# Late attention with the probabilities of seven head pairs transposed by VectorE in squares of 32 and exchanged through memory

## The reference, cut to what matters

```python
x = x + 0.5 * swiglu(rms_norm_2(x, ffn1_norm[l]), ffn1_w_gate[l], ffn1_w_up[l], ffn1_w_down[l])
h = rms_norm_2(x, mix_norm[l])
z = h @ w_in[l]
qa, ka, va, qs, ks_, vs, zg = jnp.split(z, splits, axis=-1)
...
o_na = neighbourhood_attention(qa, ka, va, na_rpb[l])
...
o_sw = sliding_window_gqa(qs, ks_, vs, t5_bias, sw_sink[l])
g = jax.nn.sigmoid((zg + b_gate[l]).astype(jnp.float32)).astype(x.dtype)
g = g.reshape(B, S, N_BRANCHES, D)
merged = g[:, :, 0] * (o_na @ w_branch_na[l]) + g[:, :, 1] * (o_sw @ w_branch_sw[l])
x = x + merged @ w_out[l]
x = x + 0.5 * swiglu(rms_norm_2(x, ffn2_norm[l]), ffn2_w_gate[l], ffn2_w_up[l], ffn2_w_down[l])
```

## Time and profile before

| | |
|---|---|
| time, median of 3 runs | 2544.74 us (2544.18 to 2547.61) |
| profiled execution | 2544.48 us |
| its span | 2543.2 us |
| mean granted clock of TensorE | 0.998 |
| TensorE busy | 2451.7 us (96%) |
| VectorE, ScalarE, GpSimd busy | 1249.2, 437.9, 178.7 us |
| moved by DMA | 712.90 MB, mean 280 GB/s |

### The profile page before, as it was taken

The page is one execution under the profiler, slowest core; times in us unless marked ns, Lnnn a source line. Parts: engine busy times, 40 slices in busy tenths (PEclk is TensorE's granted clock), DMA queues, the critical chain, the costliest instruction groups (busy, mean ns, idle before and its releaser), DMA issues.

```text
span 2543.2 us, 29763 instructions
## 1 busy us (share of the span) xinstructions
PE 2451.7 (96%) x12358; PEld 1567.5 (62%) x12358; DVE 1249.2 (49%) x2237; ACT 437.9 (17%) x1102; POOL 178.7 (7%) x126
## 2 busy tenths in 40 slices
PE   9999999888999999987889999999999999999999
PEld 5347443424578753332348866888866875888884
DVE  4994321212176621110117666545776775654774
ACT  2111110101123210000001002641101100470110
POOL 0011000000000000000000011430001003240000
PEclk9999999999999999999999999999999999999999
DMA  9854999999984499999999863415674974423671
GB/s 395 330 233 178 371 425 426 427 428 427 423 340 166 172 376 427 426 428 428 427 422 347 255 227 149 150 67 211 212 230 153 253 231 153 173 105 138 220 223 40
DMA packets 193618, 712.90 MB, mean 280 GB/s; under 512 B 117252, under 2 KB 121860, under 8 KB 128332
## 3 DMA queue, kind: packets, MB, share of 16 engines
q1 hardware_dynamic: 92304, 682.66, 67.6%
q10 hardware_dynamic: 101180, 28.35, 5.4%
HBM read 698.36 MB, written 12.60 MB: 280 GB/s over the span
## 4 chain that ended last, share of the span: by engine, by line
PE 79%; DMA 16%; DVE 4%; ACT 1%; issue 0%; POOL 0%; SPq 0%; another core or an unknown queue 0%; DVEq 0%; POOLq 0%
PE bank L867 77%; DMA ring<-in_stream 8%; DMA ring_high<-in_stream 4%; DMA ring_low<-in_stream 4%; PE bank L870 2%; DVE hidden L2892 1%; DVE ab_z L2717 1%; DMA hidden_turned<-normed 1%; DVE moe_results L2917 0%; POOL ab_ln_sum L3584 0%; DVE ring L3228 0%; DVE cd_y L2524 0%; DVE moe_turned L2913 0%; ACT normed L2243 0%; ACT hidden L2243 0%
## 5 line engine op out<-in xcount | busy, mean ns | idle before, releaser
L867 PE MATMUL bank<-ring,gates 128*128 128x256 f32 (+1 forms) x1760 | 433.6, 391 | 3.1 <-DVE ring L3228 2.1
L867 PE MATMUL bank<-ring,moe_chosen 128*64 128x512 f32 (+1 forms) x2352 | 400.3, 491 | 27.7 <-DMA ring<-in_stream 27.6
L867 PEld LDWEIGHTS bank<-ring,gates 128*128 128x128 f32 x1760 | 333.6, 190 | 70.7 <-issue 22.7
L867 PE MATMUL bank<-ring,normed 128*128 128x256 f32 x1448 | 339.6, 380 | 2.0 <-ACT normed L2328 1.3
L867 PEld LDWEIGHTS bank<-ring,moe_chosen 128*64 128x64 f32 x2352 | 150.6, 137 | 246.9 <-issue 200.4
L867 PEld LDWEIGHTS bank<-ring,normed 128*128 128x128 f32 x1448 | 273.1, 190 | 41.6 <-issue 3.9
L867 PE MATMUL bank<-normed,ring 128*128 128x256 f32 (+2 forms) x1152 | 289.8, 406 | 2.3 <-DVE normed L2698 1.5
L867 PEld LDWEIGHTS bank<-normed,ring 128*128 128x128 f32 x1152 | 189.4, 190 | 99.9 <-issue 85.4
L867 PE MATMUL bank<-ring,ffn_hidden 128*128 128x512 f32 (+1 forms) x416 | 179.3, 561 | 0.0
L2917 DVE COPY moe_results<-bank 32x512 f32<-32x512 f32 x36 | 24.8, 690 | 245.2 <-PE bank L867 244.8
L2908 DVE TENSOR_TENSOR moe_silu<-bank,moe_silu 128x512 f32<-128x512 f32 x32 | 22.1, 691 | 246.8 <-PE bank L867 246.8
(11 more groups left out here) (468 smaller groups left out, 2705.4 us busy)
## 6 DMA issues: line engine op xcount, KB each, us to landing
ring<-in_stream SPq DMA_DIRECT2D x318, 1024.0 KB, 7.3
ring<-in_stream SPq DMA_DIRECT2D x117, 2048.0 KB, 30.8
ring_low<-in_stream SPq DMA_DIRECT2D x7, 2048.0 KB, 43.8
ring_far<-in_stream SPq DMA_DIRECT2D x7, 2048.0 KB, 44.6
ring_high<-in_stream SPq DMA_DIRECT2D x6, 2048.0 KB, 44.8
hidden_turned<-normed ACTq DMA_DIRECT2D x44, 256.0 KB, 7.2
ffn_hidden<-hidden_turned ACTq DMA_DIRECT2D x44, 256.0 KB, 7.4
hidden<-in_stream SPq DMA_DIRECT2D x9, 1024.0 KB, 30.9
```

What stands on the lines that cost most here:

```text
L867: return nc.tensor.matmul(o, lhsT, rhs, start=start, stop=stop, skip_group_check=True)
```

## The change

The changed kernel no longer transposes the probabilities of pairs 0 to 6 on TensorE. `y.SC` becomes one block of 1024 columns in which the two heads' probabilities are laid out by pieces of 32 keys. After `probs(m)` VectorE transposes the whole block in squares of 32 into `y.turned`, a single buffer. SyncE then writes `y.turned` to memory in four pieces of 32 partitions and reads it back in the order of `y.PT` with two transfers (`probs_exchanged`). This stands in SyncE's order behind the refill of the place that the same pair's gate chunk has freed. The eighth pair is still transposed by TensorE. The values come three pairs after their scores (`LAG`) in place of two, and the order of VectorE's steps and that at the end of the stage are written anew. In each layer 56 transposes of TensorE and 14 copies of ScalarE go, and 7 transposes of VectorE, 28 writes and 14 reads come.

```diff
+    y.SC, y.turned = spare[:, 0:1024], spare[:, 1024:2048]
+    y.pairs = [M.ring[WEIGHT_SUMS[0]][:, SLOT + 1024 * n:SLOT + 1024 * n + 1024] for n in range(2)]
+    y.PT = [[x.rearrange("p (k i q) -> p i k q", k=TT, i=2)[:, i] for i in range(2)] for x in y.pairs]
...
+    def probs_exchanged(l, m):
+
+        sp.wait_ge(*S.vector.at(("turned_2", l, m)))
+        if m >= 2:
+            sp.wait_ge(*S.probs_in.at((l, m - 2)))
+        for q in range(4):
+            rows = bass.AP(tensor=probs_blocks[m % 2].tensor, offset=q * 32 * 1024, ap=[[128, 32], [32 * 128, 8], [1, 128]])
+            nc.sync.dma_start(rows, M.late.turned[32 * q:32 * q + 32, :].rearrange("p (k n) -> p k n", k=8)).then_inc(
+                *S.probs_out.up((l, m) if q == 3 else None))
+        sp.wait_ge(*S.probs_out.at((l, m)))
+        if m >= 2:
+            sp.wait_ge(*S.tensor.at(("values_2", l, m - 2)))
+        for k in range(TT):
+            rows = probs_blocks[m % 2].rearrange("(q k p x f) -> k p x q f", q=4, k=TT, p=P, f=32)[k]
+            to = M.late.pairs[m % 2].rearrange("p (k x q f) -> p k x q f", k=TT, q=4, f=32)[:, k]
+            nc.sync.dma_start(to, rows).then_inc(*S.probs_in.up((l, m) if k == TT - 1 else None))
+
+    gate_chunks = {ring.index["in_2", l, 9 + m] + 1: (l, m) for l in range(LAYERS) for m in range(NA_H - 1)}
...
             nc.sync.dma_start(to, src).then_inc(*ring.arrival(i).up(i if last else None))
+        if ring.to_be_free(i, n) in gate_chunks:
+            probs_exchanged(*gate_chunks.pop(ring.to_be_free(i, n)))
...
+VALUES_AT = (6,) * (NA_H - 1) + (7,)
+LAG = 3
...
-            for i in range(2):
-                pe.wait_ge(*A.at(("turned_2", l, m, i)))
+            pe.wait_ge(*(A.at(("turned_2", l, m, 1)) if m == NA_H - 1 else S.probs_in.at((l, m))))
...
         for m in range(pairs):
-            if m:
-                turned(m - 1)
             scores(m)
-            if m >= 2:
-                values(m - 2)
+            if m >= LAG:
+                values(m - LAG)
             gates_first(m)
             gates_rest(m)
             if m == 1:
                 keys_turned()
         turned(pairs - 1)
+        values(pairs - 3)
+        branch(0, 0)
+        branch(1, 0)
         values(pairs - 2)
-        branch(0, 0)
         values(pairs - 1)
-        branch(1, 0)
         branch(0, 1)
         branch(1, 1)
...
+        def turned(m):
+            dve.wait_ge(*done.at(("probs_2", l, m, 1)))
+            if m:
+                dve.wait_ge(*S.probs_out.at((l, m - 1)))
+            v.transpose(y.turned, y.SC).then_inc(*done.up(("turned_2", l, m)))
...
         for m in range(NA_H):
-            softmax(m)
+            if m:
+                gates_summed(m - 1)
+            biased(m)
+            if m:
+                gates_scaled(m - 1)
+            probs(m)
+            if m < NA_H - 1:
+                turned(m)
+            gates_first(m)
...
-            gates(m)
+        gates_summed(NA_H - 1)
+        gates_scaled(NA_H - 1)
```

More of the change, by code:

```diff
@@ L698, in wide, with probs_of, by_pieces @@
     return x.rearrange("p (o t) -> p o t", o=1).broadcast_to([P, n, x.shape[1]])
+def probs_of(y, m, i, t):
+    order = "i t k f" if m == NA_H - 1 else "k i t f"
+    return y.SC.rearrange(f"p ({order}) -> p i t k f", i=2, t=TT, f=32)[:, i, t]
+def by_pieces(x):
+    return x.rearrange("p (k f) -> p k f", f=32)
 def reversed_queries(x):
@@ L1895, in branch @@
                 pe.wait_ge(*V.at(("gated", l, p - 2, n)))
+            elif p:
+                pe.wait_ge(*A.at(("turned_2", l, NA_H - 1, n)))
             for half in range(2):
@@ L2483, in layer @@
                 keys_out()
+        values(NA_H - 3)
         turned(NA_H - 1)
+        gates(NA_H - 1)
         values(NA_H - 2)
-        gates(NA_H - 1)
         values(NA_H - 1)
@@ L3447, in keys_swapped, with biased @@
             v.tensor_copy(y.KSX[DH:P, :], y.KS[0:DH, :]).then_inc(*done.up(("ks_swapped", l)))
-        def softmax(m):
+        def biased(m):
             kind, blk = divmod(m, NA_H // 2)
@@ L3470, in softmax, with gate_parts, gates_first, gates_summed @@
                 for t in range(TT):
-                    v.tensor_scalar(y.SC[i][:, t, :], y.SC[i][:, t, :], total[:, t:t + 1], None, ALU.mult).then_inc(*done.up(("probs_2", l, m, i) if t else None))
-        def gates(c):
+                    part = probs_of(y, m, i, t)
+                    v.tensor_scalar(part, part, total[:, t:t + 1], None, ALU.mult).then_inc(*done.up(("probs_2", l, m, i) if t else None))
+        def turned(m):
[3 more added lines that the diff above has]
+            v.transpose(y.turned, y.SC).then_inc(*done.up(("turned_2", l, m)))
+        def gate_parts(c):
             b, d = (bank[x][:, :].rearrange("p (n t) -> p n t", t=P) for x in VALUES_BANK)
-            to = y.gates_of[c].rearrange("p (n t) -> p n t", t=P)
+            return b, d, y.gates_of[c].rearrange("p (n t) -> p n t", t=P)
+        def gates_first(c):
+            b, d, to = gate_parts(c)
             dve.wait_ge(*A.at(("gate_first", l, c)))
-            v.tensor_tensor(to[:, 0:4:3, :], b[:, 1:3, :], wide(to[:, 3, :], 2), ALU.add).then_inc(*done.up())
+            v.tensor_tensor(to[:, 0:4:3, :], b[:, 1:3, :], wide(to[:, 3, :], 2), ALU.add).then_inc(*done.up(("gate_firsts", l, c)))
+        def gates_summed(c):
+            b, d, to = gate_parts(c)
             dve.wait_ge(*S.chunk.at(("in_2", l, 9 + c)))
-            dve.wait_ge(*done.now())
+            dve.wait_ge(*done.at(("gate_firsts", l, c)))
             v.tensor_tensor(to[:, 1:3, :], d[:, 0:2, :], wide(to[:, 3, :], 2), ALU.add).then_inc(*done.up())
@@ L3613, in program @@
     pool_program(nc, a, M, S, ring)
-    every = [S.tensor, S.scalar, S.vector, S.pool, S.chunk, S.distance, S.spilled, S.hidden, S.sent, *S.landed, *S.into.values()]
+    every = [S.tensor, S.scalar, S.vector, S.pool, S.chunk, S.distance, S.spilled, S.hidden, S.probs_out, S.probs_in, S.sent, *S.landed, *S.into.values()]
     return {x.name: x.table for x in every}
```

39 lines of the change are left out of this document (19 added, 20 removed).

## The result

The changed kernel takes 2568.5 us (median of 5, 2565.78 to 2572.96) against 2545.1 (2544.18 to 2547.61): a ratio of 1.0094, 95% interval 1.0079 to 1.0109. It is 23.4 us slower, where 2547 was forecast and 2560 was the upper end.

What follows compares the result with a forecast made beforehand. TensorE was taken to bound the late attention stage. Per layer, -6.72 (transposes) + 1.3 (gate-sum waits) + 0.6 (end) = -4.8 us, plus 6.2 for the exchange: +1.4, both layers +2.8, so 2547 us; range 2535 to 2560.

Steps and rivals of the forecast that it cites:

- What bounds the kernel, and TensorE's saving: Late attention stage: TensorE busy for all 79.10 us; seven pairs per layer lose transposes of 0.96 us, 6.72 us per layer.
- VectorE's transpose: One square-wise transpose of 128x1024 per pair on VectorE, taken as 1.3 us.
- The waits ahead of the gate products of the second and third pair: TensorE waits there for gate sums behind VectorE's transpose: between 0 and 2.2 us per layer, taken as 1.3.
- The end: TensorE stands 0.6 us between the last values and the product needing them; a layer without the exchange comes to -4.8 us.
- The exchange: SyncE's queue round of 9.67 us holds VectorE's transpose, so TensorE waits in the fourth to eighth pair: 6.2 us per layer.
- the chunk and the writes: Terms of SyncE's queue round: 2.7 us for the ring's 1 MB chunk, 1.95 for a pair's writes of 512 KB.
- The ends of the round: SyncE's queue round sums to 9.1 us with the low ends of its terms, 10.3 with the high ends.
- The far bound: A pair's writes at the bias load's 4.4 us in place of 1.95: round 12.1, a layer +13.6, the kernel 2572.
- Forecast 2547: Whole kernel: a layer changes by +1.4 us, both by +2.8, giving 2547 us; chance 0.45.
- The rival of the slower writes: Writes from 32 partitions pass between the output's and the bias's rate: kernel 2567 at 3.9 us, 2557 halfway; chance 0.32.
- The clock: Late attention stage: the few tenths per pair that TensorE stands should leave its granted clock at 1.00.
- Pairs evenly 9.5 to 9.8 us apart: Sign of the forecast in TensorE's timeline: pairs 9.5 to 9.8 us apart; at 8.5 us they would show the hidden case.

Runs made afterwards that it cites:

- no_exchange: The changed kernel without the writes and reads of the probabilities and every wait for them: 2545.66 us, 1.0005 of the kernel before.
- tuned: The changed kernel with writes ahead of the refill, keys scaled and key halves swapped later, branch (1, 0) behind the last values: 2534.78 us, 0.9963 of the kernel before.
- small_chunk: The changed kernel with the 14 refills at the exchanges loading 32 KB in place of 1 MB: 2544.28 us, 0.9999 of the kernel before.
- busy_pe_12: The changed kernel with 12 added TensorE transposes of unused result ahead of the gate products of pairs 1 to 7: 2568.97 us, 1.0100 of the kernel before.
- reads_512: The changed kernel with the reads fetching runs of 512 B in place of 128 B: 2565.95 us, 1.0080 of the kernel before.
- early_writes: The changed kernel with each pair's writes issued ahead of the ring's refill and the reads behind it: 2543.93 us, 0.9994 of the kernel before.

## Why the prediction was wrong

- **What bounds the kernel, and TensorE's saving:** right. A pair without waits is 8.52 us (8.44 reckoned for TensorE, 8.51 for VectorE's round).
- **VectorE's transpose:** right, 1.25 us against 1.3.
- **The waits ahead of the gate products of the second and third pair:** wrong in size and in place. In no_exchange they are 1.41 us ahead of the second pair's, none ahead of the third's and 2.21 ahead of the fourth's: 3.6 us where at most 2.2 was allowed. The scaling of the keys (1.2 us) stands between the transpose and the first gate sums; with it moved, in tuned, the first of these waits is 0.37. And VectorE's operations beside GpSimd's take some four times as long. Both could be read before, the second from the probabilities of the second pair's first head, with GpSimd working beside them (those of its second head, without, take 0.62). The sum took VectorE's round from a pair without such a collision.

```profile
1623.95 1.67 DVE L3471 TENSOR_SCALAR hidden<-hidden,small 128x256 f32<-128x256 f32 x2
1624.15 1.31 POOL L3572 TENSOR_TENSOR ring<-ring,ring 128x512 f32<-128x512 f32 x1
```

- **The end:** 1.03 us against 0.6; there are two copies in a row to wait for, not one. With this the layer without the exchange is -1.3 us, not -4.8: a mis-sizing of 7 us in all. Of the 3.5 us per layer 0.8 is in none of these waits.
- **The exchange:** this is the step that failed most. The mechanism, its place and its releaser were right; the round was mis-sized, 11.94 us against 9.67 and against 10.3 with all high ends. SyncE's wake, reads and latencies were right to 0.2 us. The terms that failed are the chunk and the writes: 4.65 reckoned as a sum of mean engine times, 7.2 measured until the last packet. Of the 2.6 us between, 0.6 is the bulk and 2 the last engine, which a sum of shares over 16 engines cannot show. no_exchange puts the whole exchange at 22.8 us, median against median; 2 x 5 x 1.23 = 12.3 was reckoned.
- **The ends of the round:** added up again, the terms as they are listed give 9.3 and 10.45, not 9.1 and 10.3, and the strip of the earlier trace rows is busy for 20 slices, not 21; neither reaches the round measured. The far bound's 4.4 us comes from a stretch in which ScalarE's queue moved 0.26 MB beside the bias, which the earlier trace rows does not show.
- **"Forecast 2547":** two errors of the same sign. By medians the exchange makes 10.5 of the 21.5 us missed and the layer without it 7; the other 4 are not assigned (the profiled execution of the change lies 2.8 above its median, that of no_exchange 2.1 below). The rival of the slower writes came out near the time (2557 to 2567) but for a cause that small_chunk refutes: the writes pass at the output's rate, and what is slow is what stands ahead of them. The rule of the Trainium skill that was weighed there ("SBUF — State Buffer", section "Door 1: The DMA port swizzle (why `[64,N]` ≈ `[32,N]`)") would have an estimated 2.8 us for a pair's writes; the trace of small_chunk has 2.1, for the four sets of 32 partitions together and not for one alone, and the measurement decides.
- **The clock:** "should leave the clock alone" was wrong, it falls after waits of 4.71 and 3.94 us. The time does not feel it, by the rows of the change under busy_pe_12.
- **Pairs evenly 9.5 to 9.8 us apart:** wrong, they alternate. Pair distances in the first layer are 16.0, 8.5, 10.1 and 15.4 us: a pair that has waited long, and then begun at the lower clock, brings TensorE to the next gate products after their sums are done (1655.55, the sums at 1654.78), so that pair does not wait.

## What to carry to other kernels

Where a small transfer that someone waits for shares a queue with a large one that no one waits for, put the small one first: the order alone decided some 24 us here, with the same bytes. When a round of transfers is summed, take each from its issue to the last packet of the last engine, as it runs behind its neighbours, not its mean engine time alone. And when an engine comes within a per cent of being the bound, use its durations beside the engine that disturbs it, not the undisturbed ones.

## What the runs showed of the hardware that was not expected

- SyncE's issue of a transfer is not of fixed length. The ring's chunk took 0.33 us to issue before, 1.4 to 1.9 directly behind two reads of 2048 packets each in the change; behind reads of 512 packets each, in reads_512, 0.35 to 0.51.
- A wait of 2.21 us ahead of the same products was followed by the full clock (granted 1.00) in one layer of early_writes and by the lower one (0.51) in the other:

```profile
1641.46 2.02 PE L909 MATMUL bank<-normed,ring 128*128 128x128 f32 x16 [2.21 <-DVE ring L3538]
```

```profile
2234.03 3.65 PE L909 MATMUL bank<-normed,ring 128*128 128x128 f32 x16 [2.21 <-DVE ring L3538]
```
